# Gate and up weights of the fifth expert set in a buffer of their own

## The reference

```python
def hier_moe(h, w_rg, b_rg, w_re, b_re, w_gate, w_up, w_down):
    ...
    gsel = jnp.argmax(lg, axis=-1)                 # one of 4 groups
    ...
    top_p, top_i = lax.top_k(pe, TOP_K)            # two of its 8 experts
    ...
    eidx = gsel[:, None] * EXPERTS_PER_GROUP + top_i
    ...
    for e in range(N_EXPERTS):                     # 32 experts
        he = jax.nn.silu(hf @ w_gate[e]) * (hf @ w_up[e])
        out = out + combine[:, e:e + 1] * (he @ w_down[e])
```

## Time and profile before

| | us |
|---|---|
| median of 3 runs | 977.08 |
| lowest, highest | 975.2, 981.87 |
| the profiled execution | 976.06 |
| its span in the trace | 974.3 |

### The profile page before, as it was taken

The page is one execution under the profiler, slowest core; times in us unless marked ns, Lnnn a source line. Parts: engine busy times, 40 slices in busy tenths (PEclk is TensorE's granted clock), DMA queues, the critical chain, the costliest instruction groups (busy, mean ns, idle before and its releaser), DMA issues. The chain is left out here.

```text
span 974.3 us, 11529 instructions
## 1 busy us (share of the span) xinstructions
PE 862.8 (89%) x4738; PEld 613.3 (63%) x4738; DVE 495.0 (51%) x734; ACT 168.1 (17%) x255; POOL 150.1 (15%) x176
## 2 busy tenths in 40 slices
PE   2899999999997979899999999926999996979776
PEld 1588886347996979877666644524666664545432
DVE  1429999999999543301434425472333332222226
ACT  3211211111232121800000012100211110101003
POOL 1000000000056273201112000001222222121110
PEclk9899999999998889999999999955999998999889
DMA  9913214012323124275778392162899999999926
GB/s 321 326 47 87 80 50 173 1 43 66 90 67 96 39 55 153 102 264 196 261 276 307 101 385 99 48 259 76 357 397 419 418 415 390 374 408 396 379 105 255
DMA packets 94709, 204.12 MB, mean 210 GB/s; under 512 B 10028, under 2 KB 52372, under 8 KB 86462
## 3 DMA queue, kind: packets, MB, share of 16 engines
q1 hardware_dynamic: 69200, 134.10, 37.9%
q0 software_dynamic: 12624, 34.32, 9.6%
q10 hardware_dynamic: 12830, 34.93, 9.3%
HBM read 199.49 MB, written 14.84 MB: 220 GB/s over the span
## 5 line engine op out<-in xcount | busy, mean ns | idle before, releaser
L517 PE MATMUL PS<-arena 128*128 128x272 f32 x1024 | 240.9, 397 | 3.5 <-issue 1.9
L517 PEld LDWEIGHTS PS<-arena 128*128 128x128 f32 x1024 | 195.0, 191 | 53.8 <-issue 13.8
L1236 DVE SCALAR_TENSOR_TENSOR arena<-arena,VT 128x574 f32<-128x574 f32 x240 | 175.2, 818 | 0.0
L824 PE MATMUL PS<-arena 128*64 128x256 f32 (+1 forms) x1056 | 148.2, 410 | 29.9 <-issue 25.8
L824 PEld LDWEIGHTS PS<-arena 128*64 128x64 f32 (+1 forms) x1056 | 108.1, 156 | 65.4 <-issue 38.7
L582 PE MATMUL PS<-gH,wH 128*128 128x272 f32 x384 | 82.1, 296 | 9.2 <-POOL wL L1634 5.6
L1634 POOL TENSOR_TENSOR wL<-arena,wH 128x1024 fp32r<-128x1024 f32 x16 | 40.9, 2582 | 271.1 <-ACT wH L964 271.1
L582 PE MATMUL PS<-gL,wH 128*128 128x272 f32 x384 | 81.2, 293 | 0.0
L582 PE MATMUL PS<-gH,wL 128*128 128x272 f32 x384 | 80.9, 292 | 0.0
L1530 DVE TENSOR_TENSOR arena<-PS,arena 128x256 f32<-128x256 f32 x19 | 8.1, 425 | 139.5 <-ACT arena L1070 139.5
L844 PE MATMUL PS<-arena 128*64 128x512 f32 (+1 forms) x264 | 69.1, 597 | 1.4 <-DVE arena L1534 1.4
(11 more groups left out here) (275 smaller groups left out, 811.3 us busy)
## 6 DMA issues: line engine op xcount, KB each, us to landing
arena<-w_gate SPq DMA_DIRECT2D x32, 1024.0 KB
arena<-w_up SPq DMA_DIRECT2D x32, 1024.0 KB
arena<-w_down ACTq DMA_DIRECT2D x28, 1024.0 KB, 15.5
arena<-w_in SPq DMA_DIRECT2D x40, 512.0 KB, 5.2
arena<-w_ada SPq DMA_DIRECT2D x4, 2048.0 KB, 20.6
vecs<-w_ada POOLq DMA_DIRECT2D x4, 2048.0 KB, 9.5
arena<-w_ada POOLq DMA_DIRECT2D x4, 2048.0 KB, 8.5
arena<-x_prompt SPq DMA_DIRECT2D x8, 512.0 KB, 10.5
```

Source lines behind the costliest of these rows:

```text
L517: last = pe.matmul(PS[:, bank + h, 0:H], tile_w[:, k, :], act[:, k, h * H:(h + 1) * H], start=(k == 0), stop=(k == KT - 1))
L824: last = pe.matmul(PS[h * rows:(h + 1) * rows, 2, n * DE:(n + 1) * DE], hG[:, b, k * SLOTS + h * rows:k * SLOTS + (h + 1) * rows], buf[r / ...
L1236: dve.scalar_tensor_tensor(out=total, in0=src, scalar=tap, in1=total, op0=ALU.mult, op1=ALU.add).then_inc(conv_step, 1)
```

## The change

A fifth place for gate and up weights is added, in the first 16 KB of each partition of `vecs`, over `h2T`. Load 4 gets this place, and is issued right after `owned` and `log_ps`, ahead of the wait for `routed` and of the two `g2b` loads. Loads 5 to 31 use the four old places in turn: load n goes to place (n - 1) % 4. `gu_owner(n)` names the load whose last use it waits for: loads 5, 6, 7, 8 wait for loads 0, 1, 2, 3 (before, loads 4, 5, 6, 7 did), and from load 9 on load n waits for load n - 4 as before. In tiles: loads 5 and 6 wait for tile 1, 7 and 8 for tile 2, 9 for tile 4, 10 for tile 5. Down weights are placed and loaded as before. Inside the overflow branch SyncE gets one more wait.

```diff
--- before.py
+++ after.py
@@ -179,6 +179,8 @@
         cT32 = vecs[:, 4096:KT * T].rearrange("p (k c) -> p k c", c=NSAMPLE)
         bsb = vecs[:, 0:1024].rearrange("p (h t) -> p h t", t=P)
         bvb, vgb, vbb = (vecs[:, 1024 * n:1024 * (n + 1)] for n in (1, 2, 3))
+        WG.append([vecs[:, 0:KT * DE].rearrange("p (k n) -> p k n", n=DE)])
+        WU.append([vecs[:, KT * DE:2 * KT * DE].rearrange("p (k n) -> p k n", n=DE)])
         h2T = vecs[:, :].rearrange("p (k t) -> p k t", t=T)
         AW = [vecs[:, 0:KT * BLK].rearrange("p (k n) -> p k n", n=BLK), view(O_S, KT, BLK)]
         afb = [vecs[:, D * s:D * (s + 1)] for s in range(2)]
@@ -262,7 +264,7 @@
         routed = sem("routed")
         tokens_known = sem("tokens_known")
         own_tab, own_ps, owned = sem("own_tab"), sem("own_ps"), sem("owned")
-        gu_full = [sem(f"gu_full{r}") for r in range(4)]
+        gu_full = [sem(f"gu_full{r}") for r in range(5)]
         wd_full = [sem(f"wd_full{r}") for r in range(4)]
         g_idx, s_idx = sem("g_idx"), sem("s_idx")
         gathered = [sem("gathered0"), sem("gathered1")]
@@ -362,6 +364,16 @@
             t = min(t for t, ns in enumerate(in_tile) if n in ns)
             return 2 * (t - 1) + in_tile[t].index(n)
 
+        def gu_place(n):
+
+            return n if n < 5 else (n - 1) % 4
+
+        def gu_uses(n):
+            return 1 if n < 5 else (n - 1) // 4 + 1
+
+        def gu_owner(n):
+            return n - 5 if n < 9 else n - 4
+
         def uses(n):
             return n // 4 + 1
 
@@ -477,21 +489,24 @@
                     at = 2 * (t - 1) + h
                     load_owned(at if i is None else i * 2 + at, later(t)[0] + h)
 
+            sp.wait_ge(owned, 1)
+            sp.wait_ge(log_ps, 1)
+            load_owned(unit_of(4), gu_place(4))
             sp.wait_ge(routed, 1)
             for p in range(2):
                 sp.wait_ge(mod_stored[p], 16 * 6)
             for s in range(2):
                 sp.dma_start(g2b[s], mod_vec(5, P, s)).then_inc(g2_in, 16)
-            sp.wait_ge(owned, 1)
-            for n in range(4, LOADS):
-                sp.wait_ge(gu_done, last_use[n - 4])
-                load_owned(unit_of(n), n % 4)
+            for n in range(5, LOADS):
+                sp.wait_ge(gu_done, last_use[gu_owner(n)])
+                load_owned(unit_of(n), gu_place(n))
 
             sp.dma_start(gfb, a["g_final"].rearrange("(o n) -> o n", o=1).to_broadcast([P, D])).then_inc(fin_in, 16)
             for s, rows in ((0, P), (1, NSAMPLE)):
                 for n, dst in ((6, shfb), (7, afb)):
                     sp.dma_start(dst[s][0:rows, :], mod_vec(n, rows, s)).then_inc(fin_in, 16)
             with some_overflow(sp):
+                sp.wait_ge(gu_done, ALWAYS)
                 tiles(sp, ALWAYS + 1, TILES, over)
 
             sp.wait_ge(experts_done, 1)
@@ -802,20 +817,32 @@
                     last = pe.transpose(PS[:, k // 4, (k % 4) * SLOTS:(k % 4 + 1) * SLOTS], G[:, b, k::KT], ident[:, :])
                 last.then_inc(t_ps, 1)
 
-            def weights(i, t, full_of, per):
+            def gate_up_weights(i, t):
 
                 if t <= ALWAYS:
                     for n in in_tile[t]:
-                        pe.wait_ge(full_of[n % 4], per * uses(n))
+                        pe.wait_ge(gu_full[gu_place(n)], 32 * gu_uses(n))
+                    return [gu_place(n) for n in in_tile[t]]
+                r0, more = later(t)
+                for h in range(2):
+                    missed = 32 if r0 + h == 3 else 0
+                    pe.wait_ge(gu_full[r0 + h], cnt(i, t, 16, 16 * more - missed))
+                return [r0, r0 + 1]
+
+            def down_weights(i, t):
+
+                if t <= ALWAYS:
+                    for n in in_tile[t]:
+                        pe.wait_ge(wd_full[n % 4], 16 * uses(n))
                     return [n % 4 for n in in_tile[t]]
                 r0, more = later(t)
                 for h in range(2):
-                    pe.wait_ge(full_of[r0 + h], cnt(i, t, per // 2, per // 2 * more))
+                    pe.wait_ge(wd_full[r0 + h], cnt(i, t, 8, 8 * more))
                 return [r0, r0 + 1]
 
             def gate_up(i, t, b):
 
-                slots = weights(i, t, gu_full, 32)
+                slots = gate_up_weights(i, t)
                 pe.wait_ge(hg_ready, cnt(i, t, 2))
                 rows = SLOTS // len(slots)
                 for n, buf in enumerate((WG, WU)):
@@ -835,7 +862,7 @@
 
             def down(i, t, b):
 
-                slots = weights(i, t, wd_full, 16)
+                slots = down_weights(i, t)
                 pe.wait_ge(het_ready, cnt(i, t))
                 rows = SLOTS // len(slots)
                 for hf in range(2):
```

## The result

| | before | with the change |
|---|---|---|
| median, 20 runs each | 976.19 us | 982.81 us |
| lowest, highest | 973.89, 982.97 | 979.16, 985.51 |
| profiled span | 974.3 us | 980.8 us |

The ratio is 1.0056, 95% interval 1.0039 to 1.0072: about 5.5 us slower (3.8 to 7.0), inside the 1% that I called the limit of no change, and clear of noise. The medians lie 6.6 us apart. The forecast was 981.

The account below looks back on a forecast made before the run. Taken as bounds: `g2b` ahead of tile 1, TensorE and buffers until tile 12, then the weight stream. 976.06 + 7.0 - 3.1 = 980.0 us profiled, 981 for the median; 8 in 10 between 975.5 and 985.5.

Parts of the forecast that it names:

- Load 4 early: Ahead of the expert part: gate of load 4 is issued at about 667.8 us instead of 683.81.
- `g2b` behind it: Ahead of tile 1: `g2b`, issued at about 668.7, waits for 2.10 MB; tile 1 starts 7.0 us later, bounds 5.3 to 8.0.
- load 2's landing: Yardstick for load 4 plus `g2b`: 3.15 MB from an idle queue land 10.15 us after first issue, giving 677.95.
- the gather: Tile 3's gather, 0.54 MB on GpSimd's queue beside load 4, adds 1.3 us to `g2b`'s landing.
- the slow reading of `g2b`: `g2b` reads slower than weights, 240 GB/s; half of a possible 1.4 us, 0.7, is added to its landing.
- Everything behind tile 1 slides by the same: Owned loads wait for tiles, so the whole expert part, TensorE's and the stream's, slides by 7.0 us.
- 2.10 MB less to carry: Weight stream: 5.0 us saved, less 1.9 idle where engines run dry before load 10's issue; gain 3.1, bounds 1.6 to 5.0.
- Signs: What the profile after should show, including about 2 us of wait before tile 12 instead of 5.16.
- Whole lead: Rival: no DMA engine that matters runs dry, so the stream gains 5.0 us; median 979; chance 0.18.
- `g2b` not held up: Rival: `g2b`'s packets go beside load 4's, only its 2.2 us later issue counts; median 974 to 976; chance 0.10.
- Slower by over 1%: Rival: `g2b` behind loads takes 21.8 us, tile 1 starts 19 us later, 992 us; chance 0.05.
- the last one: Rival: load 4 isn't early because `owned` comes late, which would hold `g2b` too; 976 to 980 us; chance 0.02.

Follow-up runs that it names:

- The late wait: ScalarE waits for `g2b` only ahead of the instruction reading it: 974.90 us added to the kernel with the change, 974.86 added to the kernel before.
- the five places: Kernel with the change, plus ScalarE's later wait for `g2b`, fifth place kept in turn: up to load 14, 971.34 us; to the end, 969.25 us.
- the delay alone: Kernel before, plus an extra 2.10 MB load into `vecs`, read by nobody, ahead of `g2b`; load 4 stays where it was: 982.42 us.
- three kernels: The change as made, with `g2b` issued first, and with ScalarE's later wait: saved bytes, four places; mean 122.0 us from tile 2 to 12.
- five places always: Kernel with the change, plus ScalarE's later wait for `g2b`, with load n in place n % 5 to the end: 969.25 us, ratio 0.9929.
- `g2b` first: Kernel with the change, but the `g2b` loads are issued ahead of load 4: 977.83 us, ratio 0.9990.
- before, late wait: Kernel before, with only ScalarE's wait for `g2b` moved to the first instruction that reads it: 974.86 us, ratio 0.9980.

## Why the prediction came out as it did

*What bounds the kernel* held: `g2b` ahead of tile 1, the stream of weights from tile 12 on. The late wait and the five places each moved the one that they were aimed at.

*Load 4 early.* Issued 1.25 us after `owner`'s start; I had worked with the same. *`g2b` behind it.* Forecast 2.15 us after `owner` and a delay of 7.0, bounds 5.3 to 8.0; measured 2.19 and 6.71, and 6.77 with the delay alone. The terms were load 2's landing, the gather and the slow reading of `g2b`; the last was rough. The "possible 1.4 us" has no working: 1.05 MB at the 240 GB/s that I quoted take 4.4 us, 1.9 more than 2.5. And ScalarE's reaction came off the middle value (7.3 to 7.0) but off neither bound. The Trainium skill (DMA: Bandwidth & Descriptors, section on queues, rings and completion order) says that each DMA engine takes packets in turn from the queue rows that have work. The trace agrees as far as it goes: the gather of tile 3, issued at 672.98 behind all of load 4 and `g2b`, landed 7.9 us later, at 680.9, ahead of the second copy of `g2b`, issued at 671.2 and landed 10.1 us later, at 681.3. How much of the delay the gather costs no run isolates; 6.71 lies nearer to the sum with its 1.3 us (7.0) than to that without (5.7).

*Everything behind tile 1 slides by the same.* Nearly: tile 1 took 8.73 us instead of 9.35. I take that 0.6 us for chance. The windows above show a granted clock of 0.50 up to 685 and 0.95 from there to 690, inside this tile, and in the two runs with the late wait it took 8.45 and 10.04 us.

*2.10 MB less to carry*, gain 3.1: this is the term that was mis-sized. The rule, that the engines run dry where less is on issue, was right, and the dent ahead of load 10 came where it was forecast (730 to 740; I wrote 733 to 736). But it is deeper than I had it: 2.5 us in the mean of all engines, where I gave even the slowest one, with the most in hand, 1.9. And I looked at this one issue only. At load 11's, 11.55 us later in the kernel before, the stream dips again, by 0.45 us. The two leave 2.05 of the 5.0 us in the mean; tile 12 shows 1.1 in the kernel with the change and 1.2 in the mean of three kernels. Where the other 0.9 went no run shows, and it is within what single executions differ by. In the medians the term is smaller still: with and without the change, both with the late wait, they are equal (974.90 and 974.86). As long as TensorE sets the pace, each issue waits for a tile, and a stream that is ahead can only wait.

*Signs.* Two came out otherwise than I wrote, for the same reason: the wait before tile 12 is 4.26 us and not about 2, and tile 12's products took 8.78 us, so that nothing of the slower clock was spared.

*The way on to the end.* 2.3 us by tile 19 rather than 3.1, by the profile. After `owner` the execution with the change took 312.18 us against 307.75: 4.4 us more, where the terms gave 3.9. The 20 runs say 5.5, and 3.9 is at the low end of their interval. That 981 lies as near to the measured 982.81 as it does is in part luck: I started from a median of three runs, 977.08, and 20 give 976.19, from which the same terms lead to 980.1. A delay of 6.7 us with next to nothing won back fits the 6.6 us between the medians better than my sum does.

*Rivals.* Whole lead: excluded by the dents and by tile 12. `g2b` not held up: excluded by its landing, 9.4 us. Slower by over 1%: the interval ends at 0.72%. The load was early, so the last one falls too.

## What to carry to other kernels

Before moving a bulk load ahead of anything in a queue, look who waits for what it overtakes. Here 2.10 MB ahead of 1 MB that one engine awaited cost the expert part 6.7 us at its start and the kernel 5.5. Issuing the awaited transfer first brought the time back to that of before; waiting for it only where it is read made it 2.9 us shorter. A head start of a transfer stream can be lost again wherever a later issue has no buffer that lets it stay ahead; find each point where an issue waits for the compute side, and compare the lead with what is outstanding there, for all of them. Here five places in the turn gained time where one early load alone gained none. When part of the time varies from run to run, measure each kernel's stages from an event that all of them share.

## What I had not expected of the hardware

Gate and up of a two-expert tile take 7.13 us at the full clock. After a wait for weights they took anything from 7.13 to 10.1 us: 8.53 behind 5.16 us of idle time, 10.05 behind 5.04 in the last tile of the run with five places always:

```profile
912.90 10.05 PE L853 MATMUL PS<-arena 128*64 128x256 f32 x64 [5.04 <-issue]
```

Tile 1 varied likewise, 8.45 to 10.04 us, with equal starts 4.09 and 4.17 us after `owner` in the two runs with the late wait, each from a stretch with a granted clock of 0.50, the lower of the two levels. In the last tile nothing hides it: from the start of tile 19 to the end of the span it was 50.2 to 51.1 us in the three runs where it took 7.1 us (delay only; `g2b` first; before, late wait), and 54.2 in the two where it took 10.1. So a difference of 2 us between whole single executions says nothing here, and medians are needed.
